# Gate units over seven tiles of a head, earlier gate weights, a later far copy, and gate matmuls ahead of the transposes in a fused attention trunk

## What is computed

```python
u = rms_norm(h, norm_g[i])
# layer 0
cq, ckv, kr, g_a, q_b, k_b, v_b, g_b = split_cols(u @ ab_w_in[l], AB_SIZES)
o_a = mla_attention(...)            # 8 heads, keys of chunks <= the query's chunk
o_b = chunk_rel_attention(...)      # 8 heads, own chunk and 8 before, plus bias
mixed = concatenate([o_a * silu(g_a), o_b * silu(g_b)], -1) @ ab_w_out[l]
# layer 1
q_c, k_c, v_c, g_c, f_c = split_cols(u @ fox_w_in[l], FOX_SIZES)
o_c = forgetting_attention(...)     # 16 heads, causal, bias from a running sum
mixed = (o_c * silu(g_c)) @ fox_w_out[l]
# after each layer
h = h + mixed
h = h + (p[i] @ pe_w[i]) * sigmoid(rms_norm(h, pe_gate_norm[i]) @ pe_gate_w[i])
```

## Time and profile before

| | us |
|---|---|
| median of 3 runs (lowest, highest) | 2107.39 (2101.13, 2110.17) |
| the profiled execution | 2101.98 |
| its span, first to last instruction | 2100.1 |
| TensorE busy in the span | 1826.9 (87%) |
| VectorE, ScalarE, GpSimd busy | 979.9, 841.1, 139.9 |
| mean granted clock of TensorE | 0.929 |
| the two attention stages, from the first gate matmul | about 371 to 828 and 1422 to 1852 |

### The profile page before, as it was taken

How to read it: one execution, slowest core, us unless ns; L and a number is a source line. 1 busy time by engine, 2 the same in 40 slices (tenths; PEclk the granted TensorE clock), 3 DMA queues, 4 the chain that set the end, 5 groups by cost and what they waited for, 6 DMA issues and landing times. The chain is left out here.

```text
span 2100.1 us, 32171 instructions
## 1 busy us (share of the span) xinstructions
PE 1826.9 (87%) x12720; PEld 1665.2 (79%) x12720; DVE 979.9 (47%) x1860; ACT 841.1 (40%) x1724; POOL 139.9 (7%) x176
## 2 busy tenths in 40 slices
PE   5999876888888986999979999977888888879998
PEld 5999865777766765999979999976777777769898
DVE  5454654555544443434254444315555555552522
ACT  4432333555554544223162333315555555541510
POOL 0000000111111111000000000000111111110000
PEclk9999988899998888999999999988999989989999
DMA  5064458423333320410123334444333333141121
GB/s 170 21 215 130 131 151 217 114 72 90 92 93 78 87 63 28 173 51 26 46 101 120 121 121 142 115 115 111 81 87 91 91 91 92 41 162 55 42 78 38
DMA packets 180037, 207.18 MB, mean 99 GB/s; under 512 B 12472, under 2 KB 156104, under 8 KB 179888
## 3 DMA queue, kind: packets, MB, share of 16 engines
q1 hardware_dynamic: 178816, 201.65, 33.9%
q0 software_dynamic: 640, 2.62, 0.4%
q10 hardware_dynamic: 432, 0.85, 0.1%
HBM read 141.95 MB, written 68.90 MB: 100 GB/s over the span
## 5 line engine op out<-in xcount | busy, mean ns | idle before, releaser
L1597 PE MATMUL m_acc<-m_w_hi,g_a_hi 128*128 128x256 f32 (+1 forms) x1280 | 371.1, 290 | 19.4 <-DVE g_a_lo L1749 14.9
L1597 PE MATMUL m_acc<-m_w_hi,g_a_lo 128*128 128x256 f32 (+1 forms) x1280 | 366.0, 286 | 0.0
L1597 PE MATMUL m_acc<-m_w_lo,g_a_hi 128*128 128x256 f32 (+1 forms) x1280 | 364.0, 284 | 0.0
L1597 PEld LDWEIGHTS m_acc<-m_w_hi,g_a_hi 128*128 128x128 f32 x1280 | 245.8, 192 | 19.7 <-issue 15.0
L1597 PEld LDWEIGHTS m_acc<-m_w_lo,g_a_hi 128*128 128x128 f32 x1280 | 247.9, 194 | 0.0
L1597 PEld LDWEIGHTS m_acc<-m_w_hi,g_a_lo 128*128 128x128 f32 x1280 | 244.4, 191 | 0.0
L601 PE MATMUL pa_acc<-pa_w_hi,g_a_hi 128*128 128x256 f32 (+2 forms) x512 | 156.0, 305 | 15.9 <-DVE pa_w_lo L178 15.9
L1158 DVE TENSOR_REDUCE fox_neg_max<-fox_scores 128x1 f32<-128x128 f32 (+7 forms) x128 | 96.5, 754 | 137.5 <-PE fox_scores L1016 136.2
L1597 PE MATMUL t_acc<-t_w_hi,g_a_hi 128*128 128x256 f32 x512 | 147.6, 288 | 13.5 <-DVE g_a_lo L1749 13.5
L601 PE MATMUL pa_acc<-pa_w_hi,g_a_lo 128*128 128x256 f32 (+2 forms) x512 | 151.4, 296 | 0.0
L601 PE MATMUL pa_acc<-pa_w_lo,g_a_hi 128*128 128x256 f32 (+2 forms) x512 | 150.9, 295 | 0.0
(11 more groups left out here) (256 smaller groups left out, 4471.9 us busy)
## 6 DMA issues: line engine op xcount, KB each, us to landing
m_w_raw<-in_fox_w_in SPq DMA_DIRECT2D x12, 1024.0 KB, 6.0
ab_v<-s_v SPq DMA_DIRECT2D x16, 512.0 KB, 3.4
f_v<-g_og SPq DMA_DIRECT2D x32, 256.0 KB, 2.3
fox_q<-f_q SPq DMA_DIRECT2D x32, 256.0 KB
fox_k<-f_k SPq DMA_DIRECT2D x32, 256.0 KB
fox_v<-f_v SPq DMA_DIRECT2D x16, 512.0 KB, 3.4
pa_w_raw<-in_ab_w_in SPq DMA_DIRECT2D x6, 1024.0 KB, 5.7
s_mq<-g_og SPq DMA_DIRECT2D x32, 192.0 KB, 2.9
```

Source lines behind the costliest of these rows:

```text
L1597: last = nc.tensor.matmul(dst, a[:, k, t * P:(t + 1) * P], w[:, k0 + k, 0:n], start=(k == 0 and a is m_hi and w is w_hi), stop=(k == kt - ...
```

## The change

It has four parts, all in `stage_attention`.

- A gate unit's 24 matmuls, three per step over steps 2 to 9 of a unit, are laid into tiles 0 to 6 of the unit's own head as 4, 4, 4, 3, 3, 3, 3; tile 7 has none. In head 0 of a stage they stand in tiles 2 to 6 as 5, 5, 5, 5, 4. Tanh and `gate_times` stand at the end of tile 7 of each head.
- `load_gate` is issued one head earlier.
- ScalarE's `take_far` stands behind the evacuation and the exp of the step.
- On TensorE the gate matmuls stand ahead of the transposes of each step.

```diff
-        LATE = 2
-        def gate_unit(s):
-            f = s - LATE
-            return divmod(f, KD) if 0 <= f < KD * NH else None
+        def gate_part_of(s):
+            first = [0, 4, 8, 12, 15, 18, 21, 24, 24] if s >= NT else [0, 0, 0, 5, 10, 15, 20, 24, 24]
+            return range(first[s % NT], first[s % NT + 1]) if s < TILES else range(0)
...
                         if hd == 0:
                             load_gate(1)
-                        elif hd < NH - 1:
-                            load_gate(hd + 1)
+                        if hd < NH - 2:
+                            load_gate(hd + 2)
...
                     def gate_part(s):
-                        unit, kt = gate_unit(s)
+                        unit = s // NT
                         c, half = divmod(unit, 2)
...
+                        for n in gate_part_of(s):
+                            if n == 0:
+                                pe.wait_ge(w_lo_done, 2 * c + 2)
+                                wait(pe, g_made, unit)
+                            w, a = ((w_hi, a_hi), (w_hi, a_lo), (w_lo, a_hi))[n % 3]
+                            last = nc.tensor.matmul(gacc[:], w[:, c % 2, n // 3, :], a[:, n // 3, cols],
+                                                    start=(n == 0), stop=(n == 3 * KD - 1))
...
                             score(s)
+                        gate_part(s)
                         if 0 <= s - 2 < TILES:
                             turn_p(s - 2)
-                        if gate_unit(s) is not None:
-                            gate_part(s)
...
                     for s in range(TILES + 4):
-                        if s >= 5 and s % 2 == 1:
-                            take_far((s - 5) // 2)
                         if 0 <= s - 2 < TILES:
                             evacuate(s - 2)
                         if s < TILES:
                             exp(s)
+                        if s >= 5 and s % 2 == 1:
+                            take_far((s - 5) // 2)
...
-                        if s >= KD + LATE and (s - LATE) % KD == 0:
-                            gate_tanh((s - LATE) // KD - 1)
+                        if s < TILES and s % NT == NT - 1:
+                            gate_tanh(s // NT)
...
-                        if s >= KD + LATE and (s - LATE) % KD == 0:
-                            gate_times((s - LATE) // KD - 1)
+                        if s < TILES and s % NT == NT - 1:
+                            gate_times(s // NT)
```

More of the change, by code:

```diff
@@ L1034, in gate_part @@
                     def gate_part(s):
-                        unit, kt = gate_unit(s)
+                        unit = s // NT
                         c, half = divmod(unit, 2)
-                        if kt == 0:
-                            pe.wait_ge(w_lo_done, 2 * c + 2)
-                            wait(pe, g_made, unit)
                         cols = slice(half * HALF, (half + 1) * HALF)
[L1041 to L1046, removed]
+                        for n in gate_part_of(s):
[5 more added lines that the diff above has]
+                                                    start=(n == 0), stop=(n == 3 * KD - 1))
+                            if n == 3 * KD - 1:
+                                last.then_inc(g_summed, 1)
                     def spread_sums(uu):
```

## The result

The changed kernel is slower: 2156.41 us as a median (2152.31 to 2161.23, 4 runs) against 2104.26 us (2096.65 to 2110.17, 4 runs); the ratio is 1.0251, with a 95% interval of 1.0206 to 1.0296. The forecast was 2145, slower, range 2094 to 2184: 38 us more than before, where 52 came. The profiled executions took 2153.18 and 2101.98 us, 51.2 apart.

The account below looks back on a forecast made before the run. TensorE bounds the attention stages, busy 767 of 887 us, so its waits and clock count. Gate wait +13, removed waits -27 and late far copy +52 sum to +38: 2140 profiled, 2145 as a median, range 2094 to 2184.

Parts of the forecast that it names:

- What bounds the kernel: In the two attention stages TensorE is the bound; only what makes it wait or lowers its clock counts.
- Part 1, +13: Gate units in seven of eight tiles: the gate wait moves behind the next t = 0 scores and grows, +13 us.
- the empty tile gives no cover: Tile 7 without gate matmuls does not shorten the gate wait, whose chain starts from t = 7's scores; 3.75 us against 3.4.
- Part 3, in the -27: Gate matmuls ahead of transposes: transpose waits at t = 0 fall into the gate wait; -27 us together with earlier gate weights.
- Part 2: Gate weights one head ahead: nearly all 8.8 us of score waits and the turn waits they cause go; within the -27.
- Part 4, +52: Far half copied behind exp: L1180 comes late, so TensorE waits at the spread of the next even tile, +52 us.
- The sum, +38: All terms over the kernel: 13 - 27 + 52 = +38 us, giving 2140 profiled, 2145 as a median.
- Rival C: Slower clock: four pauses per head instead of one, 3 us more half clock each; +41, 2186 us, chance 0.17.
- The gap that repeats: Gate wait at the same place of 30 heads: by the skill's rule a missing buffer; zero or small loss, never -91.5.
- The clock's rule: Waits recurring in every tile of a loop put the clock back each time; by it the 2186 us outcome would come.

Follow-up runs that it names:

- parts 1 and 2: Kernel before with gate units over tiles 0 to 6, tanh ending tile 7, and gate weights a head earlier; transposes first, far copy first: 2008.77 us.
- part 4 alone: Kernel before with only ScalarE's far copy moved behind the exp of its step: 2119.68 us, ratio 1.0082.
- part 2 alone: Kernel before with only the gate weights loaded one head ahead: 2094.66 us, ratio 0.9947.
- change without part 4: Changed kernel with the far copy put back ahead of the evacuations: 2079.0 us, ratio 0.9893 to the kernel before.
- change without part 3: Changed kernel with the gate matmuls put back behind the transposes: 2051.77 us, ratio 0.9766 to the kernel before.
- part 1 alone: Kernel before with only gate units in tiles 0 to 6 and tanh and gate_times at the end of tile 7: 2025.19 us, ratio 0.965.
- the four with tanh early: Changed kernel with early tanh, 2029.33 us; also far copy first, 1946.5; that with transposes first, 1949.65; or with late gate weights, 1964.14.

## Why the prediction was right, and where it was not

- **What bounds the kernel.** Right: the two stages' 52.4 us are 34.9 of idle and 17.5 of busy time of TensorE, and most of the busy time is its clock. The stages before and behind changed by 1.5 us or less.
- **Part 1, +13.** In the changed kernel the walk holds: 30 waits of 3.58 to 3.71 us idle, forecast 3.6 to 3.8 lost, total 110.0 in the 95 to 115 given. But I booked the loss to the wrong part. The sentence "the empty tile gives no cover" is true only with part 3 in place. Alone, part 1 puts the scores and the seven transposes of t = 0 into the wait, which falls to 0.9 us on average, and saves 76 us. The sum of the parts came out near, and its split among them was wrong.
- **Part 3, in the -27.** The removed waits are as told (25.6 to 3.5). Its price was missing: it takes the transposes out of the cover of the gate wait, and delays the evacuation, the exp and the copy by a gate part. 70 us by itself on parts 1 and 2, and 105 with part 4. My walks had both effects inside them, since they were made with the new order; the text put them under parts 1 and 4.
- **Part 2.** The waits went as told, but not the clock. I had credited 3 us for less half clock; alone, part 2 has 24 us more of it, and its 15.1 us less idle time gave only 7 to 11 us.
- **Part 4, +52.** Right in the changed kernel in place, and 11 us too large in size, inside the bounds given: 77 waits at L1051, forecast about 90, 43.8 us of idle time, forecast 30 to 60, 26.8 of them in FoX. By tile in FoX heads, idle 0.74 at t = 2 (0.8 forecast as lost), 0.42 at t = 4 (0.8), and at t = 6 in most heads 0.94 or nothing (1.2 or 0.4). The far copy taken away gives 77 us, more than 52, since it also shortens each gate wait, by 0.75 (110.0 to 87.6 us), of which I had counted 0.6 in part 1, and lets the clock rise (228 to 191 us at half clock).
- **The sum, +38, measured +51 in the profiled executions.** Without the 3 us for the clock the forecast is 13 - 24 + 52 = +41, and the waits came to +18.5 - 22.1 + 41.0 = +37.4. That these are so near is partly luck: part 4 was taken 11 us too large and the gate wait 5.5 too small. The term that was mis-sized, with the wrong sign, is the clock. I credited 3 us for half clock removed with the load waits. There was 30 us more of it, and by the earlier trace rows at 0.43 each that is +13. With it, in place of the -3, the sum is 54. Rival C had this mechanism, at 96 us more of half clock; about a third of that came. The drains at the ends of the stages, where the turn waits are 3.0 instead of 1.6 us, are a smaller miss of the same sign.
- **The gap that repeats.** The Trainium skill (Perfetto Trace Analysis, Identifying Performance Opportunities) says that such a gap can mean a missing buffer, here a second `gacc`. The measurement shows another cause: with the same one bank and tanh early the wait is 1.5 us in all. The gap was one of order in ScalarE's list.
- **The clock's rule.** The Trainium skill (TensorE: Matmul & The Clock Gate, HAM oscillation) has a kernel in which a long wait in every turn of the loop costs the clock in every turn. For the gate wait the traces agree: 228 us at half clock with it, 56 without, the waits at the spread having grown at the same time. I had let that rule speak for rival C, whose new pauses are short; the case in the Trainium skill is one of long waits. The short waits, mostly 0.4 to 0.9 us, came with little half clock in the kernel with tanh early.

## What to carry to other kernels

When an instruction waits in a queue, ask what it stands behind, not what it reads: tanh's input was ready a tile earlier, and moving it ahead of an exp that it does not need saved 127 us without a change in the work. The same edit with the far copy first gave 1946.5 us. A filler that is moved ahead of a step's real work gives its own cover away and delays every engine behind that work. It cost 70 to 105 us while a long wait was left to cover, and nothing that could be measured once that wait was gone. So parts that look free each by itself have to be walked together, and tried in all combinations. A copy that frees a bank belongs where its engine idles waiting for that bank's writer; behind the next long instruction it becomes a link of the next chain.

## What the runs showed that I had not expected

With part 1 half of the gain came through the clock. The stages lost 38.8 us of idle time and 41.2 us of busy time, and the time at half clock fell from 198 to 102 us: 0.43 us of busy time for each, the same price as in the earlier trace rows. One kernel by itself shows a price too. By the mean granted clock, 27 executions of the kernel before have 272 to 320 us at half clock over the whole span, and 0.36 us more time for each us of it. The changed kernel's four have 318 to 337, so its 30 us more are not the scatter of one profile.

What goes with half clock is the length of the pauses rather than their sum:

| kernels | gate waits, us each (mean) | idle time of the stages, us | half clock in the stages, us |
|---|---|---|---|
| before, changed, part 4 alone, part 2 alone, change without part 4 | 2.9 to 3.7 | 141 to 193 | 191 to 228 |
| change without part 3, part 1 alone, parts 1 and 2 | 0.9 to 1.7 | 103 to 129 | 102 to 141 |
| the four with tanh early | 0.2 or less | 65 to 121 | 51 to 60 |

The kernel with tanh early and the far copy late has 121 us of idle time, with 65 us of waits at the spread and some 15 us of turn waits in pauses mostly under a microsecond, and 56 us at half clock. Parts 1 and 2 alone have 103 us of idle time and 123 us at half clock. The rule has an exception that stays open: part 2 alone took short waits away and has more half clock.

Not all of the busy time is the clock's. From the kernel with tanh early to the same with the far copy first, the waits of over 0.15 us fall from 152 to 64 and the busy time from 739.8 to 716.7 us, at 56 and 51 us of half clock: 0.26 us for each wait. Fitted to all twelve traces, the busy time goes by 0.41 us for each us at half clock and 0.29 for each wait, and misses by up to 7 us. That is an estimate. So a pause costs somewhat more than the idle time that the profile shows for it; in the prediction's walk the gate wait was 3.4 us lost and 3.25 shown.
